# Tiles 0 to 46 of expert_u by products over 512 columns, their two parts summed outside TensorE

## What is computed

```python
def _peer(h, w_query, sub_keys, expert_u, expert_v):
    ...
    v1, i1 = lax.top_k(sc[..., 0, :], PEER_TOPK)
    v2, i2 = lax.top_k(sc[..., 1, :], PEER_TOPK)
    ...
    g = jax.nn.softmax(top_s, axis=-1).astype(h.dtype)
    ...
        u = expert_u[it]
        act = jax.nn.gelu(jnp.einsum('td,tkd->tk', xt, u))
        return jnp.einsum('tk,tkd->td', gt * act, expert_v[it])
```

## Time and profile before

| | us |
|---|---|
| median of 3 runs | 1617.16 (1617.09 to 1620.21) |
| the profiled execution | 1617.7 |
| its span in the profile | 1616.1 |
| the stage of tiles 0 to 46, first product to the end of tile 46 | 895.0 to 1174.8 |

### The profile page before, as it was taken

One profiled execution on the slowest core, in us unless ns is written; L12 is line 12 of the kernel. 1 busy time (PEld: TensorE's weight loads), 2 busy tenths in 40 slices (PEclk: granted clock), 3 DMA queues, 4 the chain that ended last, 5 costly groups with the idle time before them and its releaser, 6 DMA issues.

```text
span 1616.1 us, 23533 instructions
## 1 busy us (share of the span) xinstructions
PE 1537.2 (95%) x9505; PEld 1211.5 (75%) x9505; DVE 943.0 (58%) x1600; ACT 686.5 (42%) x1032; POOL 556.0 (34%) x323
## 2 busy tenths in 40 slices
PE   7999999989889888999999999999999999999998
PEld 6789654434334333888989999999999998888886
DVE  5876422201101101777544588778777879988997
ACT  6665411101001000666452444344488865555554
POOL 4211100000000000412131443443488776888872
PEclk9999999999999999999999999999999999999999
DMA  8435999999999999645444455555544379999994
GB/s 297 153 105 185 414 401 421 421 421 421 421 421 421 421 421 411 228 145 170 131 156 144 152 194 187 176 193 195 180 155 138 122 278 332 359 359 365 360 367 168
DMA packets 99345, 444.82 MB, mean 275 GB/s; under 512 B 11152, under 2 KB 19856, under 8 KB 57632
## 3 DMA queue, kind: packets, MB, share of 16 engines
q1 hardware_dynamic: 86256, 404.90, 66.3%
q0 software_dynamic: 11264, 33.60, 5.7%
q10 hardware_dynamic: 1712, 4.76, 0.8%
HBM read 435.26 MB, written 7.86 MB: 274 GB/s over the span
## 4 chain that ended last, share of the span: by engine, by line
PE 69%; DMA 19%; DVE 6%; ACT 3%; issue 2%; POOL 0%; ACTq 0%; SPq 0%; DVEq 0%
PE ps L503 11%; PE ps L505 11%; PE ps L504 11%; PE ps L1205 11%; DMA big<-in_w_up 10%; PE ps L700 8%; PE ps L1197 7%; DMA fix<-in_w_up 3%; DMA hh<-in_w_up 3%; PE ps L1149 3%; DMA big<-in_w_down 2%; DVE fix_parts L1248 1%; PE ps L683 1%; ACT fix_parts L2142 1%; PE ps L723 1%
## 5 line engine op out<-in xcount | busy, mean ns | idle before, releaser
L2619 POOL TENSOR_TENSOR fix_parts<-fix,fix_parts 128x512 fp32r<-128x512 f32 x59 | 129.8, 2201 | 672.0 <-ACT fix_parts L2142 672.0
L505 PE MATMUL ps<-hh_parts,fix_parts 128*128 128x256 f32 x1120 | 317.5, 283 | 0.0
L700 PE MATMUL ps<-big 128*64 128x512 f32 x800 | 249.3, 595 | 17.9 <-DMA big<-in_w_up 9.5
L503 PE MATMUL ps<-hh_parts,fix_parts 128*128 128x256 f32 x768 | 219.8, 286 | 6.4 <-issue 5.5
L504 PE MATMUL ps<-hl_parts,fix_parts 128*128 128x256 f32 x768 | 218.0, 284 | 0.0
L505 PEld LDWEIGHTS ps<-hh_parts,fix_parts 128*128 128x128 f32 x1120 | 215.5, 192 | 0.0
L1248 DVE TENSOR_TENSOR fix_parts<-fix,fix_parts 128x1536 fp32r<-128x1536 f32 (+1 forms) x84 | 173.1, 2062 | 63.9 <-ACT fix_parts L2142 61.6
L700 PE MATMUL ps<-fix,big 128*64 128x512 f32 x528 | 189.4, 594 | 18.0 <-DMA big<-in_w_up 9.1
L2142 ACT ACTIVATE fix_parts<-fix 128x2048 fp32r<-128x2048 f32 x84 | 160.8, 1916 | 66.4 <-PE ps L1205 46.0
L700 PEld LDWEIGHTS ps<-big 128*64 128x64 f32 x800 | 79.7, 137 | 110.8 <-issue 109.9
L503 PEld LDWEIGHTS ps<-hh_parts,fix_parts 128*128 128x128 f32 x768 | 147.8, 192 | 7.7 <-issue 7.6
(11 more groups left out here) (420 smaller groups left out, 3661.3 us busy)
## 6 DMA issues: line engine op xcount, KB each, us to landing
fix<-in_expert_u SPq DMA_DIRECT2D x64, 1024.0 KB, 5.3
fix<-in_expert_v SPq DMA_DIRECT2D x38, 1024.0 KB, 7.6
...
```

The costliest lines, as they stand in the source:

```text
L503: pe.matmul(o, l[0], r[0], start=first, stop=False)
L505: return pe.matmul(o, l[1], r[0], start=False, stop=last)
L700: ins = pe.matmul(m.PS[64 * i:64 * i + 64, bank, :], lhs(h * k_of // 2 + k, i), view(t.place[t.slot[x]])[:, k, c0:c0 + 512], start=(h + k ...
L2619: nc.gpsimd.tensor_tensor(m.fr(x[:, at:2048]), x[:, at:2048], m.fr(hi[:, at:2048]).bitcast(F32), ALU.subtract).then_inc(s.lo_g, 1)
```

## The change

- For tiles 0 to 46 TensorE makes, for each `j` and `k`, one product of 512 columns (the high part of the weights by both token parts, which now lie beside each other in `m.HX`), and one of 256 columns (the low part of the weights by the high token part) into columns 0 to 255 of the same bank. Each `j` has a bank of its own, so a tile has two: 4 and 5, or 2 and 3. Columns 256 to 511 hold the part that must still be added. From tile 47 on the three products of 256 columns stay, in bank 4 or 7.
- ScalarE copies columns 0 to 255 (`u_copy`) to `m.ST` and `m.W`, VectorE adds columns 256 to 511 (`u_sum`), and ScalarE then applies the gelu in place. In step `i` this is done for tile `i - 1`.
- TensorE waits for `u_sum` instead of the gelu before it takes a bank again.
- On VectorE the first routing item of a step now stands ahead of `u_sum` and of the low part, the others behind them.
- For tiles 0 to 46 VectorE takes 1280 columns of the low part (`U_SHARE`) and GpSimd 768.
- The semaphore `fold` is merged with `parts`.

```diff
+U_SHARE = 1280
...
+def u_banks(i):
+
+    return ((4, 5), (2, 3) if i < MAPS_AT else (7, 7))[i % 2]
...
+def u_half(m, i, x):
+
+    one, two = u_banks(i)
+    at = m.PS[:, one, 256 * x:256 * x + 1]
+    return bass.AP(at.tensor, at.offset, [at.ap[0], [512 * (two - one), 2], [1, 256]])
...
-    m.HT = (fr(m.HH[:, :, :]), fr(m.HL[:, :, :]))
+    m.HX = nc.alloc_sbuf_tensor_at("hx", [P, 2, 8, 256], FR, offset=nc.sbuf_base - 4 * 4096)
+    m.HT = (m.HX[:, 0, :, :], m.HX[:, 1, :, :])
...
-        bank = 4 + i % 2
+        banks = u_banks(i)
         if i < 2:
             pe.wait_ge(s.sc, 8)
+        elif i < MAPS_AT + 2:
+            pe.wait_ge(s.u_sum, i - 1)
         else:
             pe.wait_ge(s.act, i - 1)
         for j in range(2):
             for k in range(8):
                 at = 1024 * j + 128 * k
-                ins = pe_pass3(pe, m.PS[:, bank, 256 * j:256 * j + 256], [x[:, at:at + P] for x in (hi, lo)],
+                if i < MAPS_AT:
+                    pe.matmul(m.PS[:, banks[j], :], hi[:, at:at + P], m.HX[:, :, k, :], start=(k == 0), stop=False, skip_group_check=True)
+                    ins = pe.matmul(m.PS[:, banks[j], 0:256], lo[:, at:at + P], m.HX[:, 0, k, :], start=False, stop=(k == 7),
+                                    skip_group_check=True)
+                    continue
...
-    return SHARE if n < t.split[t.first["expert_v"]] else 2048
+    first = t.split[t.first["expert_u"]]
+    if n >= first + 64:
+        return 2048
+    return U_SHARE if first <= n < first + MAPS_AT else SHARE
...
+    def u_sum(i):
+        ve.wait_ge(s.u_half, i + 1)
+        src = u_half(m, i, 1)
+        ve.tensor_tensor(m.ST[i % 2], src[:, :, 0:SPARSE], m.ST[i % 2], ALU.add)
+        w = m.W[:, 2 * i:2 * i + 2, :]
+        ve.tensor_tensor(w, src[:, :, SPARSE:256], w, ALU.add).then_inc(s.u_sum, 1)
...
+        route = ROUTING.get(i, [])
+        for what, b, n in route[:1]:
+            dve_route(nc, m, s, v, what, b, n)
+        if 0 < i <= MAPS_AT:
+            u_sum(i - 1)
         dve_low(nc, m, s, t, first + i + 1)
...
-        for what, b, n in ROUTING.get(i, ()):
+        for what, b, n in route[1:]:
             dve_route(nc, m, s, v, what, b, n)
...
+    def u_copy(i):
+        ac.wait_ge(s.used, t.used[f["expert_u"] + i])
+        if i >= 2:
+            ac.wait_ge(s.acts_kept[i % 2], 16 * (i // 2))
+        src = u_half(m, i, 0)
+        ac.activation(m.ST[i % 2], src[:, :, 0:SPARSE], ACT.Copy)
+        ac.activation(m.W[:, 2 * i:2 * i + 2, :], src[:, :, SPARSE:256], ACT.Copy).then_inc(s.u_half, 1)
+
     for i in range(64):
+        if 0 < i <= MAPS_AT:
+            u_copy(i - 1)
         act_high(nc, m, s, t, first + i + 1)
...
+        if 0 < i <= MAPS_AT:
+            ac.wait_ge(s.u_sum, i)
+            ac.activation(m.ST[(i - 1) % 2], m.ST[(i - 1) % 2], ACT.Gelu_apprx_tanh)
+            w = m.W[:, 2 * i - 2:2 * i, :]
+            ac.activation(w, w, ACT.Gelu_apprx_tanh).then_inc(s.act, 1)
         for what, b, _ in ROUTING.get(i, ()):
...
+        if i < MAPS_AT:
+            continue
...
-    at = SHARE
+    at = share_of(t, n)
```

14 lines of the change are left out of this document (7 added, 7 removed).

## The result

The changed kernel takes **1624.95 us** (median of 7 runs, 1621.40 to 1627.93), the kernel before in the same session 1618.11 us (7 runs, 1614.77 to 1620.21). The ratio is 1.0048, 95% interval 1.0037 to 1.0059: slower by some 7 us, where 2.5 us less were forecast. The result lies outside the range given (1610.5 to 1621.5) and on the other side of no change. The profiled execution took 1626.13 us. Its span is 1624.5 us, its mean granted clock 0.996.

The account below looks back on a forecast made before the run. TensorE was taken to set the pace, with a chain over ScalarE, VectorE and GpSimd as long. Terms -0.7 - 2.5 - 0.6 - 0.3 + 1.2 + 0.4 = -2.5 us gave 1614.7 us; range 1610.5 to 1621.5.

Parts of the forecast that it names:

- TensorE's tile and the chain: Tiles 0 to 46: TensorE alone would take 5.54 us, the chain sets 5.75 instead of 5.765; -0.7 us over 45 tiles.
- rival D: Products of 512 columns reading two places of `hx` run slower; at 0.24 us nothing changes; no chance of its own given.
- GpSimd's 768 columns: GpSimd's low part in tiles 0 to 46: taken as 1.75 us, between 1.71 and 1.85.
- The gates: Exponentials of routing: VectorE makes `gates` first, the second table load falls into idle time behind the high part; -2.5 us.
- Heads: Two heads between low parts make a tile some 0.9 us late, partly made up by the next; +1.2 us for both blocks.
- Selections: VectorE's additions over SBUF wait for GpSimd's longer instruction; +0.2 us each, +0.4 us in all.
- The sparse lists: ScalarE's wait and TensorE's 3.0 us wait stay; `keys` goes ahead of the low part; -0.3 us.
- The transposes: After tiles 22 and 45, 0.4 us each, falling partly into TensorE's new idle time; -0.6 us.
- The additions: VectorE's two additions from PSUM in each tile: 0.67 us, hidden by ScalarE's high part.
- Rival B: VectorE's additions out of PSUM also keep GpSimd out: +9 us over 27 tiles, 1623.5 us; chance 0.06.
- Rival C: VectorE becomes the bound, its list tiles having 0.25 us left: +7 us over 34 routing tiles, 1621.5 us; chance 0.10.

Follow-up runs that it names:

- before_share1280: Kernel before with one edit: VectorE takes 1280 columns of the low part and GpSimd 768 in tiles 0 to 46; 1623.79 us, ratio 1.0043.
- after_small_adds: Changed kernel with VectorE's two additions of a tile cut to one of 128x8, leaving out most of the sum; 1617.45 us, ratio 1.0001.
- after_exp_first: Changed kernel with the exponential of the gates moved ahead of ScalarE's wait for the sum and its gelu; 1621.73 us, ratio 1.0025.
- after_1536_side_by_side: Changed kernel, VectorE at 1536 columns, gates' exponential and sparse-list issue one tile later, routing behind the low part, token halves side by side per row block; 1612.19 us.
- after_1536_small_adds: Changed kernel with VectorE's share back at 1536 columns and its two additions cut to one of 128x8; 1613.38 us, ratio 0.9962.
- after_share1536: Changed kernel with VectorE's share back to 1536 columns, GpSimd 512; 1616.27 us, ratio 0.9997.

## Why the prediction was wrong

The forecast was 2.5 us less, and 6.8 us more were measured. Two steps carry most of the difference: that TensorE's own tile was in hand beside the chain, and that the stall at the exponentials would vanish, since VectorE would make `gates` ahead of it.

**TensorE's tile and the chain: mis-sized, and the reason to call it harmless was wrong.** The forecast summed two tiles as 5.54 + 0.20 + 5.76. The chain came out at 5.78. TensorE's tile came out at 5.66, and at 5.73 where the first pair was slow too (0.43 us at 912.93). The forecast had looked at slower products in rival D and written that "at 0.24 us a product nothing changes, since TensorE has 0.2 us a tile in hand". The product takes 0.23 to 0.24 us, and it changed the result: in its own sum TensorE's tile stands beside the chain and not under it, once for every two tiles. In the trace the two tiles are 11.71 us and not 11.50: 0.12 us from the pace of the pairs, 0.07 from the slow first pair, 0.02 from the chain. That is 0.1 us a tile, 2.7 us over the 26 intervals of the first row of the table, of a miss of 3.4. The first tiles add to it (intervals 2 and 3 of the changed kernel take 6.05 and 6.31 us).

**GpSimd's 768 columns: mis-sized a little.** Forecast 1.75, measured 1.84 to 1.88 alone and 1.80 behind VectorE. The 1.80 lies between the 1.75 taken and the 1.85 that proportion gives, the upper end of the range. before_share1280 shows what the share costs by itself: +6.8 us in the stage of the kernel before. The forecast had no such number, since it set the loss in the chain off against TensorE's gain in one step. Its way of adding, with GpSimd at 1.85, gives 5.92 us a tile for this case, and the trace has 5.91. Undone in the changed kernel, the same edit gives back 6.9 us in the stage and 8.7 us in the medians.

**The gates: right mechanism, wrong order of events.** The step said that VectorE makes `gates` first and the exponential then costs nothing. It named ScalarE's order, but overlooked that the exponential stands behind a gelu that is now VectorE's to release. VectorE is nearly a tile behind after the heads, so ScalarE's wait of 1.92 us for `gates` became one of 2.87 us for the sums. after_small_adds and after_exp_first both take the loss away, from VectorE's end and from ScalarE's.

**Heads: mis-sized by half.** +1.2 forecast, +2.57 measured. The forecast let the next tile make part of it up. With two heads every second step and 0.65 to 0.7 us of sums in each, there is nothing to make it up with. Cutting the sums brings it to +0.66; changing the share doesn't move it (+2.62).

**Selections: mis-sized.** +0.4 forecast. One group of eight multiplications, 6.06 us instead of 2.76, is 3.3 us more by itself; it met GpSimd's instruction twice.

**The sparse lists** were about right, +0.25 for -0.3. The same wait stayed, 3.8 us. The transposes can't be told apart in this trace.

**The additions** were sized right: 0.71 us from 914.34 to 915.05, and 0.65 us between 980.20 and 980.85, for 0.67. Rival B is refuted: GpSimd's 768 columns took 1.84 us at 974.84 with an addition of 0.55 us wholly beside them, as long as in before_share1280, which has no additions (1.84 to 1.85 us alone), and cutting the additions changes nothing in the list tiles. That its 1623.5 us lie nearest to the measured time is luck. Rival C, with 1621.5 us and 0.10 of the chance, had more of the mechanism. It holds in the tiles with heads, gates and selections, and not in the list tiles that it named first: VectorE still had 0.87 us idle there at 921.35. Rival D named slower products, and they came, but not by the two places of `hx`, as after_1536_side_by_side shows, and the sentence that they change nothing was wrong. The chance on slower, 0.19, was too small, because the sum set two gains that rested on an engine being in time against losses that made this engine late.

One sum of the range doesn't come out: GpSimd at 1.71 and heads at nothing give -1.6 - 2.5 - 0.6 - 0.3 = -5.0 us, not -5.5. The lower end played no part in the result.

How much each part is to blame has no single answer, since the two overlap. Taking away the share's change gives 8.7 us and cutting the sums 7.5 us, and the whole loss is 6.8. Either is enough to bring the kernel back to that before; both together (after_1536_small_adds) give 11.6 us between the medians, 13.9 by the ratios. What the products of 512 columns bring with the old share is the -2.13 us of after_share1536 in 26 tiles, 0.08 us a tile, where 0.22 had been put for TensorE alone. The chain still takes its part there: by the forecast's way of adding, 5.66 + 0.20 + 5.53 us for two tiles, 5.69 us each (an estimate), and the 26 tiles have 5.70.
